# Hybrid decoder trunk on one core: the two heads of a pair in one slot of the hand-made schedule

## What is computed

```python
for layer in range(DEPTH):
    u = rmsnorm(h, attn_norm[layer])
    (mla_dq, mla_dkv, mla_kr, gla_q, ..., gate_logits) = jnp.split(u @ w_in[layer], offsets, axis=-1)
    o_mla = mla_branch(...)      # q, k: up-projection, rmsnorm per head, rope; softmax(q k^T) v, causal
    o_gla = gla_branch(...)      # chunked linear attention with decay, rmsnorm per head, gated
    o_hgrn = hgrn2_branch(...)   # the same form with other gates
    gates = jax.nn.sigmoid(gate_logits).reshape(B, L, N_BRANCH, D_MODEL)
    mixed = (gates[:, :, 0] * (o_mla @ w_mla_o[layer])
             + gates[:, :, 1] * (o_gla @ w_gla_o[layer])
             + gates[:, :, 2] * (o_hgrn @ w_hgrn_o[layer]))
    h = h + mixed @ w_out[layer]
    ...
```

## Time and profile before

| what | value |
|---|---|
| median of 3 runs | 1955.93 us (1954.07 to 1957.28) |
| profiled execution, its own time | 1951.37 us |
| its span | 1949.5 us, 30232 instructions |
| TensorE busy | 1865.6 us, 96% |
| VectorE busy | 1538.6 us, 79% |
| ScalarE busy | 1294.5 us, 66% |
| mean granted clock of TensorE | 0.990 |

### The profile page before, as it was taken

How to read it: one execution, slowest core, us unless ns; L and a number is a source line. 1 busy time by engine, 2 the same in 40 slices (tenths; PEclk the granted TensorE clock), 3 DMA queues, 4 the chain that set the end, 5 groups by cost and what they waited for, 6 DMA issues and landing times.

```text
span 1949.5 us, 30232 instructions
## 1 busy us (share of the span) xinstructions
PE 1865.6 (96%) x11056; PEld 1620.7 (83%) x11056; DVE 1538.6 (79%) x1898; ACT 1294.5 (66%) x1640; POOL 43.1 (2%) x42
## 2 busy tenths in 40 slices
PE   7998999999979998999899999999999999999998
PEld 6988888899978887888788888888888888888886
DVE  5868787555438688776898998989989889798897
ACT  5776766444336775864676777767777677776775
POOL 0000003000000000012000000000000000000001
PEclk9999999999999999999999999999999999999999
DMA  5323324455443332336499998989989999998994
GB/s 190 130 92 126 108 98 142 141 174 173 160 176 108 114 116 96 119 120 242 170 370 347 352 371 331 369 350 355 367 350 356 346 353 371 351 349 346 357 369 171
DMA packets 83702, 474.14 MB, mean 243 GB/s; under 512 B 10480, under 2 KB 10768, under 8 KB 40352
## 3 DMA queue, kind: packets, MB, share of 16 engines
q1 hardware_dynamic: 83616, 472.98, 65.0%
HBM read 471.89 MB, written 1.05 MB: 243 GB/s over the span
## 4 chain that ended last, share of the span: by engine, by line
PE 73%; DVE 12%; ACT 9%; issue 5%; DMA 1%; POOL 0%; DVEq 0%; ACTq 0%; SPq 0%; POOLq 0%
PE bank L1690 9%; PE bank L1695 9%; PE bank L1691 9%; PE bank L1414 8%; PE bank L1416 7%; PE bank L1415 7%; PE bank L1707 5%; PE bank L1713 5%; PE bank L1708 5%; DVE mlo L1211 2%; DVE lo L872 2%; PE bank L1659 1%; ACT hi L593 1%; PE bank L1722 1%; PE bank L1409 1%
## 5 line engine op out<-in xcount | busy, mean ns | idle before, releaser
L1211 DVE TENSOR_TENSOR mlo<-mraw,mhi 128x2048 fp32r<-128x2048 f32 x283 | 642.2, 2287 | 70.3 <-ACT mhi L806 69.3
L806 ACT ACTIVATE mhi<-mraw 128x2048 fp32r<-128x2048 f32 x283 | 539.6, 1916 | 104.6 <-PE bank L1695 53.9
L1414 PE MATMUL bank<-UH,hi 128*128 128x272 f32 (+1 forms) x1376 | 416.4, 303 | 18.8 <-DVE UL L885 8.6
L1416 PE MATMUL bank<-UH,lo 128*128 128x272 f32 (+1 forms) x1376 | 397.5, 289 | 0.0
L1415 PE MATMUL bank<-UL,hi 128*128 128x272 f32 (+1 forms) x1376 | 396.2, 288 | 0.0
L593 ACT ACTIVATE hi<-raw 128x1024 fp32r<-128x1024 f32 (+1 forms) x220 | 229.3, 1043 | 133.0 <-PE bank L1416 123.9
L1690 PE MATMUL bank<-mhi,xh 128*128 128x512 f32 x768 | 303.3, 395 | 3.4 <-DVE xl L1296 3.4
L1691 PE MATMUL bank<-mhi,xl 128*128 128x512 f32 x768 | 299.9, 390 | 0.0
L872 DVE TENSOR_TENSOR lo<-raw,hi 128x1024 fp32r<-128x1024 f32 (+1 forms) x220 | 266.2, 1223 | 41.6 <-ACT hi L593 41.1
L1414 PEld LDWEIGHTS bank<-UH,hi 128*128 128x128 f32 x1376 | 260.7, 189 | 32.9 <-issue 27.3
L1415 PEld LDWEIGHTS bank<-UL,hi 128*128 128x128 f32 x1376 | 261.8, 190 | 1.6 <-issue 0.5
(11 more groups left out here) (342 smaller groups left out, 2584.5 us busy)
## 6 DMA issues: line engine op xcount, KB each, us to landing
mraw<-in_w_exp SPq DMA_DIRECT2D x336, 1024.0 KB, 4.8
raw<-in_w_dense SPq DMA_DIRECT2D x212, 512.0 KB, 3.2
raw<-in_w_dense SPq DMA_DIRECT2D x8, 384.0 KB, 3.0
wuq<-in_w_uq SPq DMA_DIRECT2D x2, 1024.0 KB, 7.2
mixed<-in_x SPq DMA_DIRECT2D x2, 512.0 KB, 5.9
wukv<-in_w_ukv SPq DMA_DIRECT2D x2, 512.0 KB, 7.6
out<-acc SPq DMA_DIRECT2D x4, 256.0 KB, 3.0
C<-in_consts SPq DMA_DIRECT2D x1, 576.0 KB, 7.9
```

Source lines behind the costliest of these rows:

```text
L806: A_(mhi[k % MHI][:], mraw[k % MRAW][:], ACT.Copy).then_inc(mhi_made, 1)
L1211: TT(mlo[k % MRAW][:], mraw[k % MRAW][:], mhi[k % MHI][:].bitcast(F32), ALU.subtract).then_inc(mlo_made, 1)
L1414: MM(ps, h, xh_, start=first, stop=False)
L1416: return MM(ps, l, xh_, start=False, stop=last)
```

## The change

Three things in the two functions that make the schedule.

In `la_steps` the steps `a`, `o` and `n` of a mixer's second head take the slot of the first. In `build_schedule` the attention steps of one layer were 46 entries spread evenly over the slots between `gd` and the last `wo`; now the same step of both heads of a pair is one entry, `ss`, `vm` and `pv` are one each, and these 26 entries are spread over the same slots. So the slots of layer 0 become: qk of heads 0 and 1 at 17, nrm at 21, sc at 26, rc at 30, pt at 35, pv at 39; nrm of heads 2 and 3 at 48, sc at 53, rc at 57, pt at 62, pv at 66; qk of heads 4 and 5 at 71, nrm at 75, sc at 80, pt at 89, pv at 93; qk of heads 6 and 7 at 98, nrm at 102, sc at 107, pt at 116, pv at 120. The `a` steps of unit 1 are at 77 and its `o` steps at 79, those of unit 2 at 105 and 107. `vm` moves from slot 10 to 12. `LATE`, the steps' contents and all waits stay.

```diff
--- before.py
+++ after.py
@@ -182,7 +182,7 @@
     head = late + 5
     for h in range(0, 4 if unit == 0 else 2, 2):
         for s in ("a", "o", "n"):
-            at += [(s, h, head), (s, h + 1, head + 1)]
+            at += [(s, h, head), (s, h + 1, head)]
             head += 2
     return [((3 * layer + unit, s, i), n) for s, i, n in at]
 
@@ -207,11 +207,16 @@
 
         at = 2 * (g0 + kinds.index(("gd", 0))) + 2
         end = 2 * (g0 + kinds.index(("wo", 11))) + 1
-        heads = [s for s in mla if s[1] != "ot"]
-        for n, s in enumerate(heads):
-            side.setdefault(at + n * (end - at) // len(heads), []).append(s)
-        for s in mla[len(heads):]:
-            side.setdefault(end + s[2] // 2, []).append(s)
+        groups = []
+        for s in mla:
+            if s[1] in ("ss", "vm", "pv") or s[1] != "ot" and s[2] % 2 == 0:
+                groups.append([s])
+            elif s[1] != "ot":
+                groups[-1].append(s)
+            else:
+                side.setdefault(end + s[2] // 2, []).append(s)
+        for n, group in enumerate(groups):
+            side.setdefault(at + n * (end - at) // len(groups), []).extend(group)
 
         for unit, first in enumerate((("gd", 0), ("f", 0), ("f", 2))):
             for s, n in la_steps(layer, unit):
```

## The result

The changed kernel takes 1998.4 us (median of 4 runs, 1997.03 to 2000.59), the kernel before on the same chip 1955.66 (4 runs, 1954.07 to 1957.28): the ratio is 1.0223, 95% interval 1.0207 to 1.0238. The forecast was 1978, range 1964 to 1997. The sign was right and so was the place; the loss is twice the one forecast. The profiled execution of the kernel before was a quick one (1951.4 us at a mean granted clock of 0.990, where the 42 executions that stand beside the experiments have a median of 1955.5 us at 0.985), so the two profiles lie 46.7 us apart and the medians 42.7.

The account below looks back on a forecast made before the run. TensorE was taken to bound the kernel, with VectorE's order deciding its waits in the attention layers. Waits of 20.2 us plus 4 for the clock minus 2 for switches gave +22 on the 1955.9 median: 1978 us, range 1964 to 1997.

Parts of the forecast that it names:

- `o` of unit 1: Heads 4 and 5: TensorE's o step would wait 4.3 us for the AT mask, queued behind two nrm on VectorE.
- `ds` of unit 2: Heads 6 and 7: ds would wait 2.6 us in place of 1.3, the last kt copy starting later.
- job 37: Heads 4 and 5: this streamed job's bank evacuation would follow two qk and three kt copies, coming 0.8 us later.
- the second `sc`: Heads 0 and 1: TensorE would want this step at 76.5 and wait 2.8 us behind VectorE's nrm block.
- Job 27: Heads 2 and 3: this streamed job would start 4.6 us later, near 154.2, its evacuation standing behind both nrm.
- Rivals 1 and 2: First: slack absorbs the blocks, 1956 us, chance 0.08. Second: fewer waits and switches make it faster, 1948 us, chance 0.07.
- the +3.0 of heads 2 and 3: Net delay in us forecast for this pair in layer 0, after later waits of 0.8 and 0.8 vanish; bounds +1 and +6.
- rival 2: Faster: vanished waits for L718 and L1002 and 2 to 8 us of switches give 1947 to 1950; chance 0.07.
- `a` of unit 2: Heads 6 and 7: TensorE's a step would wait 5.4 us for the S update, queued behind the nrm block on VectorE.
- the term for the clock: Attention layers: long new waits drop TensorE's granted clock, four times 1.7 us less two existing stretches: +4, bounds 0 and +10.
- Rival 3: Slower still: some 12 waits at 1.7 us of clock loss are 20 in place of 7; 1991 to 1997, chance 0.20.
- The small term: TensorE, both layers: forty fewer switches between streamed and side work would save 2 us, bounds 0 to 8.

Follow-up runs that it names:

- e3: The changed kernel, with VectorE alone doing the second head's nrm two slots later; TensorE's and ScalarE's orders kept: 1974.86 us, ratio 1.0114.
- e5: The kernel before, with five unread additions (2.3 us) on VectorE ahead of unit 1's first AT mask in each layer: 1961.63 us, ratio 1.0038.
- e6: The kernel before, with nine unread additions (4.2 us) on VectorE ahead of unit 1's first AT mask in each layer: 1969.52 us, ratio 1.0076.
- e1: The kernel before, with only the mixers' a, o and n steps of two heads sharing a slot; attention keeps its 46 entries: 1955.39 us, ratio 1.0003.
- e4: The changed kernel, with filler matmuls nobody reads put into four TensorE waits per layer: 1977.66 us, ratio 1.0139.
- e7: The changed kernel, with 32 filler matmuls per layer at one place alone, ahead of unit 1's first o: 1989.26 us, ratio 1.0171.

## Why the prediction was wrong, and where it was right

**What holds.** At least half of the loss comes by VectorE's order: e3 changes that order alone and halves it, and its longest waits still end on VectorE. TensorE's waits were forecast at +20.2 us for both layers and are +20.5. Point by point, as layer 0 / layer 1, forecast in front: `o` of unit 1 4.3, measured 4.0 / 4.3; `ds` of unit 2 2.6, measured 2.4 / 2.6; job 37 released 0.8 us later, and its wait is 2.5 / 2.6 in place of 1.7; the second `sc` 2.8, measured 1.7 / 2.0. Job 27 was to start near 154.2 and starts at 154.87; of the delay 3.1 us stands at `sc` of head 3 and 1.7 at the job itself, where I had looked for one long wait. The wait for L718 is gone, that for L1002 down by 1.2, VectorE's busy total is nearly unchanged (1542.2), the `nrm` block is 8.4 us as worked out. Rivals 1 and 2 fall with this. Two sums of the prediction don't come out of their own terms: the +3.0 of heads 2 and 3 (6.2 - 0.9 - 0.8 - 0.8 is 3.7), and rival 2's 1947 to 1950, since its 8 us of switches would have given 1941.5.

The agreement of the sum is partly luck: `a` of unit 2 was forecast at 5.4 us and is 2.2 in layer 0, 5.2 in layer 1. In layer 0 TensorE came to `a` after 10.2 us at the lower clock (279.6 to 289.8), in layer 1 after 3.4; 6.8 us more at half rate is 3.4 us, about the difference. That is argued from the trace, not tried. It also shows how the two losses mix: a slow TensorE comes late to its next wait and finds it shorter, so waits and clock can't be forecast apart.

**The step that failed** is the term for the clock: "The new waits of 4.3 and 5.8 us per layer have no later wait to absorb this: 4 times 1.7 is 6.8", less what existed, "+4, bounds 0 and +10". It measured 26.2 us between the profiled executions, about 22 between the medians. Two things were far too small in it. *How many*: I priced two waits per layer, though I named four to eight dips as the sign; the trace has five low stretches in layer 0 and six in layer 1, since waits of 1.7 to 3.1 us drop the clock too. *How long*: I took 3.5 us for each, from rows 9, where the waits were of 1.3 and 2.05 us. Behind the new ones the stretches are 3.4, 6.8 or 10.2 us, and e5 and e6 show 6.8 and up to 13.7 us from one block on its own. So the sum had some 7 us more at the lower level, where the profiles show 71.7. The price of each such us was not too small: 1.7 for 3.5 is 0.49, and 0.37 stayed as time. Rival 3 put this at 20 us ("some 12 waits at 1.7"): nearly the right count, and half the length; with it the sum gave 1991 to 1997, and 1998.4 lies just above. Both numbers of rows 9 were right; what was wrong was to carry the price of a 1.3 us and a 2 us wait over to waits twice as long, and to leave out the shorter ones.

**The small term** that failed too: fewer switches were to save 2 us. Run e1 merges 24 pairs of steps, which takes away 20 of the 40 switches; its idle time is within 1.1 us of before in each layer, and its time differs by 0.03%, less than its interval. The rows say why. Timeline of PE in the changed kernel, two `nrm` merged:

```profile
138.30 0.62 PE L1496 MATMUL bank<-qsq,C 96*96 96x272 f32 x2
...
139.22 0.62 PE L1496 MATMUL bank<-qsq,C 96*96 96x272 f32 x2
...
139.94 0.49 PE L1419 MATMUL bank<-UH,hi 128*128 128x272 f32 x1
```

The next stream starts 1.64 us after the first `nrm` matmul; one `nrm` alone takes TensorE 0.72 us in the kernel before (62.14 to 62.86). Two together are not cheaper than twice one, so the switch had no price to save. Of the bounds given (0 to 8 us) zero is the value, which is worth 2 us of the miss.

**The sum again** with the measured terms: +20.5 for waits, +26.2 for the clock, 0 for switches, 46.7 of span between the profiled executions; between the medians 20.5 and about 22, 42.7, against 22 forecast. The mean granted clock agrees with the 22: from 0.985 to 0.970 over some 1976 us is 59 us more at half rate, and 59 times 0.37 is 22, an estimate.

**What stays open.** Why the clock fell for 6.8 us behind one wait of 4.3 us and for 13.7 behind another of 4.5 in the same kernel. Low stretches differ from one execution to the next of the same kernel (the spread of the kernel before, the fourth execution of e4), and each profile here is of one execution. The fillers in e4 sit in four places only, so that the waits for KLT and `mixed`, 2.4 and 3.5 us in layer 0, were never filled.

## What to carry to other kernels

Two equal steps put into one slot save TensorE nothing, but queue as one block on the engine behind it; look for who stands behind that block, and give each pair of steps a split or an evacuation between them. Where TensorE is the bound, price a wait of 2 to 4 us above its length; in this kernel the two waits made on purpose cost 1.5 to 1.7 times their length over all executions. Compare low-clock time over several executions before it is put down to an edit. Read a wait list as a list of moves and move one step at a time: the `pv` steps moved by one slot and two `qk` per layer by two on VectorE gave 0.5%, and one more move in the same run had hidden it.

## What the runs showed of the hardware that I had not expected

The clock's price lies behind the wait, in work that looks healthy: from 222 to 232 us TensorE was busy 9.72 of 10 us, at a clock of 0.51 and with 42 records where e7 has 73. Stretches at the lower level come in sizes of 3.4, 6.8, 10.2 and up to 17.1 us, and their size doesn't follow from the wait alone: 2.4 us (at KLT in layer 0 of the changed kernel) was followed by 10.2, 4.0 by 10.2, 4.3 by 6.8, 4.5 by 13.7. Nor is it fixed for a kernel: the same one ran with a mean granted clock of 0.983 in one execution and 0.991 in another, 10 us apart.

The Trainium skill, "TensorE: Matmul & The Clock Gate", section "Part 1: The HAM clock gate (the "warmup" mystery)", puts the penalty of the ramp to the full clock, for modelling, at under 1% of a typical span, and says so of the warm-up at a kernel's start. Carried over to a kernel that falls back many times, it would give under 19.5 us of 1949.5, an estimate. It does not carry over: here the falls behind waits cost 26.2 us or 1.3%. The section "HAM oscillation — how this bites in real kernels" of that page holds that a kernel with repeated idle gaps pays the return to the full clock again and again; the trace agrees, with eleven stretches in the two mixer stages.

Matmuls that compute nothing can pay: 32 in one wait of 4 us per layer gave 9.1 us over two layers, and 117 per layer in four waits gave 20.7.
